# One more request for the table set with logarithm and exponential, behind the last tile of z

## The reference

```
x = layer_norm(x)
h = x @ w_in                       # split: qkv, z, gates a and b, and q, k, v of the attention
o_gdn = gated_delta(l2norm(silu(conv(q))), l2norm(silu(conv(k))), silu(conv(v)), exp/softplus/sigmoid of a, b)
o_gdn = rms_norm(o_gdn_forward + o_gdn_backward) * silu(z)
o_na  = rms_norm(softmax(q k^T / 8 + bias) v)      # each token attends to a window of 8 x 16 on a 16 x 64 grid
x = layer_norm(alpha x + [o_gdn, o_na] @ w_out)
x = layer_norm(alpha x + relu(x @ w1 + b1)^2 @ w2 + b2)
```

## Time and profile before

| what | value |
|---|---|
| median of three | 4017.76 us (4017.4, 4017.76, 4025.91) |
| profiled execution, its own time | 4014.57 us |
| its span in the profile | 4012.8 us |
| mean granted TensorE clock | 0.983 of full speed |
| busy: TensorE, DVE, ACT | 3868.0, 2219.4, 1631.8 us |
| ACT_TABLE_LOAD, all | 1283 ns each |
| TensorE in the mixers, 415 to 906 us | 442.88 of 491 us busy, clock 0.90 |

### The profile page before, as it was taken

The page is one execution under the profiler, slowest core; times in us unless marked ns, Lnnn a source line. Parts: engine busy times, 40 slices in busy tenths (PEclk is TensorE's granted clock), DMA queues, the critical chain, the costliest instruction groups (busy, mean ns, idle before and its releaser), DMA issues.

```text
span 4012.8 us, 49119 instructions
## 1 busy us (share of the span) xinstructions
PE 3868.0 (96%) x20396; PEld 3118.1 (78%) x20396; DVE 2219.4 (55%) x3368; ACT 1631.8 (41%) x2546; POOL 17.1 (0%) x34
## 2 busy tenths in 40 slices
PE   4999999989999999999999999999999999999999
PEld 2777777777788787878778878977777877778887
DVE  6541666666633556765658746346646346546333
ACT  3351455665433453443534335233335233334333
POOL 0000000000000000000000000000000000000000
PEclk9999988999999999999999999999999999999999
DMA  4112000013242222222222222222222222223222
GB/s 169 48 58 75 10 7 6 24 60 107 81 119 95 95 90 81 77 84 95 84 88 76 90 89 90 85 90 79 79 89 90 90 89 79 79 90 116 95 94 85
DMA packets 113876, 323.56 MB, mean 81 GB/s; under 512 B 26920, under 2 KB 34040, under 8 KB 113656
## 3 DMA queue, kind: packets, MB, share of 16 engines
q1 hardware_dynamic: 111416, 314.91, 23.9%
q0 software_dynamic: 2240, 5.51, 0.7%
HBM read 303.86 MB, written 18.06 MB: 80 GB/s over the span
## 4 chain that ended last, share of the span: by engine, by line
PE 88%; DVE 6%; ACT 4%; issue 1%; DMA 0%; SPq 0%; DVEq 0%; ACTq 0%
PE ps L311 50%; PE ps L289 26%; PE ps L1351 2%; PE ps L1037 1%; PE ps L725 1%; PE ps L2466 1%; PE ps L1328 1%; PE ps L1336 1%; PE ps L1905 1%; PE ps L1031 1%; DVE g_D L1233 1%; PE ps L421 1%; ACT g_dec L1176 0%; DVE n_s L1441 0%; DVE g_R L1261 0%
## 5 line engine op out<-in xcount | busy, mean ns | idle before, releaser
L311 PE MATMUL ps<-a,w_hi 128*128 128x512 f32 (+1 forms) x6128 | 1876.8, 391 | 9.0 <-DVE a L508 6.5
L311 PEld LDWEIGHTS ps<-a,w_hi 128*128 128x128 f32 x6128 | 1127.6, 189 | 282.1 <-issue 23.3
L311 PE MATMUL ps<-a,w_lo 128*128 128x512 f32 (+1 forms) x3064 | 1163.6, 386 | 0.0
L262 DVE TENSOR_TENSOR w_lo<-w_raw,w_hi 128x1024 fp32r<-128x1024 f32 x539 | 657.9, 1221 | 449.2 <-ACT w_hi L257 446.4
L257 ACT ACTIVATE w_hi<-w_raw 128x1024 fp32r<-128x1024 f32 x539 | 563.8, 1050 | 544.3 <-DMA w_raw<-in_w_mlp 342.4
L311 PEld LDWEIGHTS ps<-a,w_lo 128*128 128x128 f32 x3064 | 571.5, 189 | 122.9
L289 PE MATMUL ps<-h_hi,w_hi 128*128 128x512 f32 x1536 | 490.4, 401 | 1.9 <-DVE xT L361 1.9
L289 PE MATMUL ps<-h_hi,w_lo 128*128 128x512 f32 x1536 | 481.5, 395 | 0.0
L289 PE MATMUL ps<-h_lo,w_hi 128*128 128x512 f32 x1536 | 481.2, 395 | 0.0
L356 DVE TENSOR_TENSOR h_lo<-u_sq,h_hi 128x512 fp32r<-128x512 f32 x192 | 133.0, 693 | 492.8 <-ACT h_hi L346 492.7
L361 DVE TENSOR_TENSOR xT<-xT,ps 128x1024 f32<-128x1024 f32 x192 | 234.1, 1219 | 287.7 <-PE ps L289 287.0
(11 more groups left out here) (362 smaller groups left out, 3265.0 us busy)
## 6 DMA issues: line engine op xcount, KB each, us to landing
w_raw<-in_w_mlp SPq DMA_DIRECT2D x384, 512.0 KB, 3.3
w_raw<-in_w_in SPq DMA_DIRECT2D x107, 512.0 KB, 3.3
w_raw<-in_w_out SPq DMA_DIRECT2D x48, 512.0 KB, 3.3
xT<-in_x SPq DMA_DIRECT2D x2, 2048.0 KB, 12.6
x<-xT SPq DMA_DIRECT2D x2, 2048.0 KB, 7.6
xT<-x SPq DMA_DIRECT2D x2, 2048.0 KB, 10.1
rpb_rows<-in_rpb SPq DMA_DIRECT2D x1, 3810.0 KB
z<-staged SPq DMA_DIRECT2D x4, 512.0 KB, 3.7
```

The source lines that it names most:

```text
L262: nc.vector.tensor_tensor(w_lo[u.z][:, :], w_raw[u.z][:, :], w_hi[u.z][:, :].bitcast(F32), ALU.subtract).then_inc(w_split[u.z], 1)
L311: last = nc.tensor.matmul(ps[:, bank, 0:t1 - t0], w[:, k * P:(k + 1) * P], a[:, h, low, k, t0:t1], start=(i_k == 0 and i == 0), stop=(i_k ...
```

## The change

ACT requests LOG_EXP once more, right behind the eviction of the last z tile (`u.j == GH - 1`, GH = 4). Nothing else changes: the same activations, waits, DMAs and buffers.

```
@@ -703,6 +703,8 @@
                 act.wait_ge(stored, 16 * u.nth)
             func = ACT.Silu if u.kind == "z1" else ACT.Copy
             nc.scalar.activation(staged[:, :], banks(u.bank), func).then_inc(bank_free(u), 1)
+            if u.kind == "z1" and u.j == GH - 1:
+                act.preload_act_table_set(LOG_EXP)
 
         def nk1_act(act, u):
             if u.j == 0:
```

## The result

The changed kernel takes 3975.03 us (median of four, 3970.55 to 3975.98) against 4017.58 us before: 42.5 us less, a ratio of 0.9887 with a 95% interval of 0.9870 to 0.9904. The direction and the place of the gain are as forecast; the size is not. (The four executions lie between 3970.55 and 3975.98, so the edge is missed by less than they spread; the forecast itself is missed by 12 us.)

The account below looks back on a forecast made before the run. TensorE, busy 96%, was taken as the bound, so ACT's loads matter only where TensorE waits. Loads 14.6 us (6.0 + 5.1 + 0.9 + 2.57) plus clock 16 gave 30.6 us less than 4017.8: 3987 us, range 3976 to 4006 (own range 3976 to 3995).

Parts of the forecast that it names:

- the clock: Six half-clock stretches of TensorE behind rows where DVE waits for ACT, 4.0 us each: four come back, 16 us.
- The rival that nothing is removed: Loads are placed without regard to the set requested, so the 60 stay: 4018 us or 1.3 more; chance 0.03.
- (b): Five attention rows, called exposed, where DVE idles for ACT's loads: TensorE gains 1.2 us each, 6.0 us in all.
- (c): Two rows where DVE waits for ACT, sharing a slot with an output norm: 2.57 us each, 5.1 in all.
- Heads, layer norms: Loads in the heads (260 to 370 us) and at L425/L427: hidden behind TensorE's other work, 0 us.
- (a): Eight attention rows, called covered, where ACT finishes before DVE needs the result, 2 us to spare: 0 us.
- norms 5 to 7: Output norms behind the last attention row: TensorE works through prepared half units meanwhile, so 0 us.
- (d): Three rows with hidden loads and an output norm: DVE's wait of 0.44 us at L1521 saved in two, 0.9 us.
- (e): Last attention row, with nothing left beside it to hide the loads: 2.57 us gained.
- Loads only: Rival: clock still falls behind rows where DVE waits for ACT, two stretches or fewer return: 3995 to 4006 us; chance 0.27.
- DVE takes over: Rival: DVE's own chain limits the rows without a norm; 8.6 us gained, no clock, 4009 us; chance 0.06.
- slower: Rival: shorter steps bring new clock falls, 4.0 us each; with seven, 4031 us; chance 0.04.

Follow-up runs that it names:

- experiment 2: The changed kernel with two loads put back in each of the eight covered attention rows, 16 in all: 3978.11 us.
- experiment 6: The changed kernel with the seventeen loads outside the loop put back (last head, output norms 5 to 7, layer norms): 3975.75 us.
- experiment 3: The kernel before, all 60 loads in place, with eight filler matmuls per delta-rule step ahead of L1037's wait behind an exposed row: 3997.87 us.
- experiment 9: The changed kernel measured once more, with nothing altered: 3974.54 us.
- experiment 1: The changed kernel with two loads put back in each of the eight exposed attention rows, 16 in all: 4012.41 us.
- experiment 4: The changed kernel with one load put back in each of the eight exposed attention rows, in front of Ln: 3977.10 us.
- experiment 10: The changed kernel with the splits of the first two output weights moved behind the last row's norm on ACT and DVE: 3974.10 us.
- experiment 5: The changed kernel with the ten loads of the five output norms in the loop put back: 3993.38 us.

## Why the prediction was right in its mechanism and wrong in its size

In one sentence first: what the loads themselves cost was right, the step that failed is the clock, of which I took 16 us (four falls of six) where 21.3 came back (six of six), and nothing for the covered rows' falls, where 5.8 us more came back.

- *What is removed.* Right: 60 loads gone, one new one, ACT 77.9 us less busy (75.7 worked out). The rival that nothing is removed is refuted by the groups of ACT. (The Trainium skill's rule of the longest run, "ScalarE activation tables: per-element evaluation and per-set limits", section "Table sets in the compiler and the runtime", would have left the time as it was; the trace disagrees, with 60 loads gone.)
- *The price of a load.* Right: with 1283 ns the waits of (b) and (c) came out to a tenth or two. The activation behind L707 starts 1.29 us after it, with nothing between. (The drain of 1380 ns that the Trainium skill adds, "ScalarE: Activation LUTs", section "What ACT_TABLE_LOAD costs", shows in no row of this case.)
- *Heads, layer norms, covered rows (a), norms 5 to 7: nothing.* Right, by experiments 2 and 6.
- *Exposed rows (b), 1.2 us each.* Right in every step of the chain, 1.22 to 1.24 us a row as read, and confirmed by the one load that costs nothing. By experiment 3 it is 1.5 us at most.
- *Norms (c), 2.57 us each.* Right in size: 26.23 to 23.53 us in the row whose clock had not fallen, 2.7. But it is two waits and not one: the first L1336 of that row waited for ACT as well, behind the load of L1514, which neither nor the working has. It went from 2.01 to 0.58 us, the second L1336's from 1.78 to 0.50.

```profile
790.10 1.09 PE L1336 MATMUL ps<-consts,n_s 128*128 128x128 f32 x8 [2.01 <-ACT g_vt L1514]
```

- *Covered rows with a norm (d), 0.44 us in two.* One of them can be read without the clock: the step from 811.36 took 32.52 us and takes 31.99, 0.5 less. The other lies in the last step.
- *The last row (e), 2.57.* The step shrank by 1.6 us: ACT now waits 1.84 us for a weight's DMA ahead of its splits, 0.93 before. The clock is in it too; in experiment 9 the same step shrank by 2.9.
- *The loads together, 14.6 us.* By the table: 6.2 to 7.5 in the five rows, 5.4 (two norms at 2.7), the last row 1.6 and 0.5 of part (d), 13.7 to 15.0 us.
- *The clock, "four of six = 16".* Here it failed. All six stretches came back: 17.5 us in the five rows and 3.8 in the one with a norm (29.98 - 23.52 less 2.7), 21.3; with the direct reading of the wait it is 22.6. My ground for holding two back was that the row at 786 kept its clock behind an idle time of 1.78 us. That showed only that an idle time does not always bring a fall. It said nothing on whether a fall would come without one.
- *"The covered rows have falls of their own ...; those stay."* Wrong: of six, three were shorter and one gone, and the covered steps lost 6.3 us, of which I had 0.5. The clock is what a covered step varies by: with some 6.8 us at half clock it takes 33.5 to 34.4 us in these two profiles, with some 3.3 us 32.5 to 32.8. Why the falls are shorter is not settled. The idle times ahead of them are the same (1.34 to 1.35 us in four of the rows before and after). The seven covered steps add up to 232.0 to 233.1 us in the three profiles with both loads in the exposed rows and no filler behind the covered ones (before, experiments 1 and 3), to 226.8 to 229.2 in the six with at most one load there, none at the norms in the loop and no filler (after, experiments 2, 4, 6, 9 and 10). Since experiment 3 has its clock at 1.00 behind every exposed row, it is not the exposed rows' falls that lengthen the covered ones.
- *The range.* With all six and the loads in full my own bounds gave 4017.8 - 24 - 21.5 = 3972. I ended the range at 3976, which treated the two bounds as if both could not be near. With all six and the loads as forecast the sum is 4017.8 - 24 - 14.6 = 3979, inside the range; it took the covered rows as well to leave it. Besides, the profiled execution was 3 us faster than the median, and the falls of the clock that it happened to have were taken for what the kernel has.
- *The rivals.* "Loads only" is refuted by the clock of all exposed rows; "DVE takes over" by L1039 starting with L1338; "slower" did not happen.

## What to carry to other kernels

Ask of every wait on the critical engine what the engine does after it: here the idle time of 1.2 us cost less than the 7 to 10 us at half clock that it brought (2.5 to 4.4 us a row), and of the gain 13.1 us were idle time and 26.0 us the clock. Price a delay by the slack ahead of it and not by its length: one load in each exposed row cost nothing that could be told from the spread, two cost 35 to 37 us. Where Ln and Exp alternate, request the set with both behind the last function that is in neither, and look in the trace for alternating loads.

## What the runs showed of the hardware that was not expected

- A kernel with all its loads in place became 21.9 us faster by useless matmuls in an idle time of 1.2 us (experiment 3): the clock stayed at 2.4 GHz instead of falling to 1.2 GHz for 7 to 10 us.
- The same program has a low clock in some executions and not in others at the same place: 430 to 442 us at 0.57 in experiment 2 and at 1.00 in the changed kernel, with the same code up to there. A fall has no fixed length either: behind idle times of 1.34 to 1.35 us in covered rows the kernel before has some 6.8, 3.3, 6.7 and 3.2 us at half clock. In 27 executions of the kernel before, in the three groups of experiments, the times lie between 4014.46 and 4025.35 us.
- A request for a table set that is already loaded costs the full 1283 ns again (experiments 1, 2, 4 to 6).
